# Two-layer hybrid trunk on one core: layers written out without barriers, opening transpositions one group late, output projection begun chunk by chunk

## The reference

```python
def _layer(x, mod, p, states):
    sh1, sc1, g1, sh2, sc2, g2, sh3, sc3, g3 = split(mod, 9)
    x = LN(ALPHA*x + 0.5*g1*swiglu(x*(1+sc1)+sh1, ffn_w_gu[0], ffn_w_down[0]))
    y, new_states = token_mixer(x*(1+sc2)+sh2, p, states)
    x = LN(ALPHA*x + g2*y)
    x = LN(ALPHA*x + 0.5*g3*swiglu(x*(1+sc3)+sh3, ffn_w_gu[1], ffn_w_down[1]))
    return x, new_states

# token_mixer: u = hin @ w_in feeds three branches (HGRN2, mLSTM, SSD); then
proj = einsum('blcr,crd->blcd', stack([y_hg, y_ml, y_mb]), w_branch)
y = einsum('blcd,de->ble', sigmoid(bg) * proj, w_out)

mod = silu(c) @ w_mod + b_mod     # 9 vectors of 1024 for each layer and token group
```

## Time and profile before

| | us |
|---|---|
| median of 3 runs | 2666.69 |
| the runs | 2666.21 to 2667.34 |
| the profiled execution | 2667.78 |
| span of that execution, first to last instruction | 2666.0 |

### The profile page before, as it was taken

The page is one execution under the profiler, slowest core; times in us unless marked ns, Lnnn a source line. Parts: engine busy times, 40 slices in busy tenths (PEclk is TensorE's granted clock), DMA queues, the critical chain, the costliest instruction groups (busy, mean ns, idle before and its releaser), DMA issues. The chain is left out here.

```text
span 2666.0 us, 36350 instructions
## 1 busy us (share of the span) xinstructions
PE 2397.3 (90%) x13210; PEld 2199.8 (83%) x13210; DVE 1201.2 (45%) x1684; ACT 1055.2 (40%) x1637; POOL 1472.8 (55%) x620
## 2 busy tenths in 40 slices
PE   4999989998889988999949999899988898889995
PEld 1999979787866787999949989788967678879995
DVE  3544137473643373542145431476637335554412
ACT  4443345333353625322244433642344445252222
POOL 3777645664364753655438775456634556445551
PEclk8999989999988998999979999899999899989998
DMA  6455333343243431443315543333323343323331
GB/s 228 145 172 173 124 97 135 111 135 119 77 134 122 157 95 64 146 127 115 130 47 182 166 153 124 109 119 127 119 97 109 135 134 127 103 89 127 125 118 55
DMA packets 96891, 331.26 MB, mean 124 GB/s; under 512 B 11248, under 2 KB 16624, under 8 KB 96368
## 3 DMA queue, kind: packets, MB, share of 16 engines
q1 hardware_dynamic: 89424, 320.41, 36.3%
q10 hardware_dynamic: 7328, 8.97, 1.0%
HBM read 325.14 MB, written 4.20 MB: 124 GB/s over the span
## 5 line engine op out<-in xcount | busy, mean ns | idle before, releaser
L540 POOL TENSOR_TENSOR wlo<-raw,whi 128x1024 fp32r<-128x1024 f32 (+2 forms) x616 | 1472.6, 2407 | 1144.9 <-ACT whi L1014 1112.0
L1014 ACT CAST whi<-raw 128x1024 fp32r<-128x1024 f32 (+1 forms) x616 | 632.3, 1038 | 838.5 <-DMA raw<-in_w_f 202.2
L573 PE MATMUL ps<-h_hi,whi 128*128 128x384 f32 x2176 | 748.8, 344 | 30.4 <-DVE xs L1620 13.3
L575 PE MATMUL ps<-h_hi,wlo 128*128 128x384 f32 x2176 | 737.3, 339 | 0.0
L574 PE MATMUL ps<-h_lo,whi 128*128 128x384 f32 x2176 | 736.6, 338 | 0.0
L573 PEld LDWEIGHTS ps<-h_hi,whi 128*128 128x128 f32 x2176 | 416.5, 191 | 49.2 <-issue 35.7
L574 PEld LDWEIGHTS ps<-h_lo,whi 128*128 128x128 f32 x2176 | 415.6, 191 | 6.3 <-issue 1.6
L575 PEld LDWEIGHTS ps<-h_hi,wlo 128*128 128x128 f32 x2176 | 415.1, 191 | 0.0
L573 PE MATMUL ps<-act_hi,whi 128*128 128x384 f32 x704 | 239.6, 340 | 11.8 <-DVEq L490 11.8
L575 PE MATMUL ps<-act_hi,wlo 128*128 128x384 f32 x704 | 239.3, 340 | 0.0
L574 PE MATMUL ps<-act_lo,whi 128*128 128x384 f32 x704 | 239.2, 340 | 0.0
(11 more groups left out here) (284 smaller groups left out, 3003.5 us busy)
## 6 DMA issues: line engine op xcount, KB each, us to landing
raw<-in_w_in SPq DMA_DIRECT2D x240, 512.0 KB, 3.5
raw<-in_w_f SPq DMA_DIRECT2D x136, 512.0 KB, 3.5
raw<-in_w_gu SPq DMA_DIRECT2D x88, 512.0 KB, 3.4
raw<-in_w_down SPq DMA_DIRECT2D x64, 512.0 KB, 3.4
raw<-in_w_down SPq DMA_DIRECT2D x32, 384.0 KB, 3.0
raw<-in_w_branch SPq DMA_DIRECT2D x24, 512.0 KB, 3.5
raw<-in_w_mod SPq DMA_DIRECT2D x16, 512.0 KB, 5.1
raw<-in_w_out SPq DMA_DIRECT2D x16, 512.0 KB, 3.4
```

Of the source, the lines that this page charges most:

```text
L540: nc.gpsimd.tensor_tensor(wlo[s][:, 0:w], raw[s][:, 0:w], whi[s][:, 0:w].bitcast(F32), ALU.subtract).then_inc(w_split, 1)
L573: mm(out, hi_, xh[:, xc, :], start=start and n == 0, stop=False)
L575: last = mm(out, lo_, xh[:, xc, :], start=False, stop=stop and n == len(chunks) - 1)
L1014: act.copy(whi[s][:, 0:w], raw[s][:, 0:w]).then_inc(w_hi, 1)
```

## The change

1. **Layers written out.** The loop over layers is a Python loop in each stream. The semaphores are not cleared; each wait adds what a layer has added before (`passed`). `layer_over` and the meeting ahead of it are gone. The third layer norm of layer 0 is followed at once by the modulated input of layer 1 with folded factors, as the other two are, and `ahead` runs across the border. The parameters of both layers are loaded at the start. y is stored chunk by chunk behind the affine step.
2. **Opening.** The rows of the four groups alternate between PSUM banks 0 and 1 and two row buffers. PE turns group g-1 behind the products of group g, ACT copies it after two more roundings. ACT also rounds the first four units of the layer in the opening, and a fifth after the second chunk's modulated input.
3. **Branches and output projection.** DVE makes `h_hi` straight from the sum, with the halving in it, for both chunks, then both `h_lo`. The factors (`adaln`) are made ahead of block 1, not of block 3. The first two units of the output projection go to banks 4 and 5, chunk by chunk, each chunk waiting only for its own `h_lo`.

```diff
-            with act.Fori(0, L) as l:
-                step.n = 0
-                act.dma_start(par[:, :], ins["par"][l]).then_inc(par_loaded, 16)
-                for k in range(AHEAD + 1):
-                    ahead(l, k - AHEAD)
-                act.wait_ge(md_go, 1)
-                for n in range(KC):
-                    modulated(0, n, mod[:, KC:2 * KC, :], mod[:, 0:KC, :])
+            for l in range(L):
+                now["l"] = l
+                if l == 0:
+                    act.wait_ge(md_go, 1)
+                    for n in range(KC):
+                        modulated(0, n, mod[:, KC:2 * KC, :], mod[:, 0:KC, :])
+                        if n == 1:
+                            ahead(l, 0)
                 ffn(l, 0, UF1)
...
                 layer_norm(l, 2)
-                meet(act, MEET["end", 0])
-                layer_over(act, l, "act")
...
@@ ACT, layer_norm
-                if j < 2:
-                    ahead(l, (UM, UF2)[j])
+                follows = j < 2 or l < L - 1
+                if follows:
+                    ahead(l, (UM, UF2, U_SPLIT)[j])
...
                 for n in range(KC):
                     act.wait_ge(ln_out, KC * j + n + 1 + passed(ln_out))
-                    if j < 2:
+                    if follows:
                         modulated(j + 1, n, gs, bs)
...
@@ PE, opening
-                mod_product(ps[0], m % NSET, m % 4).then_inc(w_used, 1)
-                if m % 4 == 3:
-                    pe.wait_ge(rows0_out, i(4) + (m // 4 + 1))
...
+            for m in range(U_MOD0):
+                pe.wait_ge(w_split, m + 1)
+                mod_product(ps[m // 4 % 2], m % NSET, m % 4).then_inc(w_used, 1)
+                if m % 4 == 3 and m > 3:
+                    first_turn(m // 4 - 1)
+            first_turn(U_MOD0 // 4 - 1)
...
@@ ACT, opening
+            for m in range(U_MOD0):
+                k = m + AHEAD
+                round_unit(k // NSET, k % NSET)
+                if m % 4 == 1 and m > 4:
+                    first_row(m // 4 - 1)
+            first_row(U_MOD0 // 4 - 1)
...
@@ PE, output projection
-                pe.wait_ge(br_hi, KC)
-                for k in range(U_OUT):
+                for c in range(KC):
+                    pe.wait_ge(br_hi, c + 1 + passed(br_hi))
+                    for m in range(2):
+                        if c == 0:
+                            unit_split(pe, l, u0 + m)
+                        last = block_product(ps[OUT_BANKS[m]][:, 0:T], u0 + m, h_hi, h_lo, [(c, c)], c == 0, c == KC - 1)
...
@@ DVE, branches
-                    if mblk == 3:
+                    if mblk == 1:
...
-                    ts(z[:, :, :], z[:, :, :], 0.5, None, ALU.mult).then_inc(br_z2, 1)
-                    dve.wait_ge(br_z2, mblk + 1)
-                    for j in range(2):
-                        k = 2 * mblk + j
-                        step(cp(h_hi[:, k, :], z[:, j, :]))
-                        step.done()
-                        tt(h_lo[:, k, :], z[:, j, :], h_hi[:, k, :].bitcast(F32),
-                           ALU.subtract).then_inc(br_hi, 1)
+                    ks = (2 * mblk, 2 * mblk + 1)
+                    for j, k in enumerate(ks):
+                        step(ts(h_hi[:, k, :], z[:, j, :], 0.5, None, ALU.mult))
+                    step.done()
+                    for j, k in enumerate(ks):
+                        stt(h_lo[:, k, :], z[:, j, :], 0.5, h_hi[:, k, :].bitcast(F32), ALU.mult,
+                            ALU.subtract).then_inc(br_hi, 1)
...
@@ SP, end
-            sp.wait_ge(layer_end, 9 * L)
-            sp.dma_start(outs["y"], x[:, :, :]).then_inc(stored, 16)
+            for n in range(KC):
+                sp.wait_ge(x_out, n + 1)
+                sp.dma_start(outs["y"][:, n, :], x[:, n, :]).then_inc(stored, 16)
```

473 lines of the change are left out of this document (239 added, 234 removed).

## The result

| | before | after |
|---|---|---|
| median, us | 2667.02 (4 runs, 2666.21 to 2670.44) | 2600.64 (4 runs, 2591.33 to 2605.78) |
| ratio to before | | 0.9745, 95% interval 0.9715 to 0.9775 |
| profiled execution, its span | 2667.78, 2666.0 | 2598.43, 2596.6 |
| mean granted clock | 0.943 | 0.955 |

What follows compares the result with a forecast made beforehand. PE, busy 90% of the span, was taken as the bound, so only its pauses and the slow clock behind them pay. Terms 25.1 + 14 + 24.6 + 5.5 = 69.2 us gave 2597.5, range 2589 to 2610.

Steps and rivals of the forecast that it cites:

- The border, 25.1: Between the layers: affine step, meeting, clearing, reload and five roundings leave the path, 25.1 us, bounds 22 and 27.
- The opening, 14: Start to first product: late turns and moved roundings let PE start at 52 to 53, not 66.45; 14 us, bounds 9, 18.
- 4.1 us more: Opening, behind the last row's copy: five roundings gone from there, 4.1 us on top of the 9 from an earlier copy.
- The rival of the weight ring: Opening: engines and DMA hang on each other through six buffers, gain 5 instead of 14, total 2606.5; chance 0.10.
- Branches and output projection, 24.6: Both layers: shorter waits and less lost clock around the branches, 12.3 us a layer, 24.6 in all, bounds 17 and 28.
- The output projection: Behind the branches: 36 matmuls with ready inputs cover PE's wait of 4.81, plus 1.7 of clock; gain 6.5 us a layer.
- Block 3: In the branches: without adaln PE's wait falls from 4.45 to 0.4, plus 1.8 of clock; gain 5.9 us a layer.
- Block 1: In the branches: adaln is new ahead of it; one blocked VectorE instruction as before, and 0.1 us more a layer.
- the first rival: VectorE late at block 1: blocked instructions and lost clock cost (2.1 + 1.8) x 2 = 8 us, total 2605; chance 0.10.
- The end, 5.5: Store of y: the last of eight small stores lands about 2.7 us after issue; 5.5 us gained, bounds 4 and 6.
- the prediction's own sign: Among PE's waits: a new entry over 3 us, above all for POOL's wlo in opening or border, would show it wrong.
- Straight code starves a sequencer: Rival on the written-out layers: late instruction fetch stops PE, 117 us over 87 packets, total 2715; chance 0.03.

Runs made afterwards that it cites:

- experiment 3: Two kernels, each the change with one edit: last row copied ahead of rounding unit 19 (2599.91 us), or VectorE's table work behind its last four units (2593.57 us).
- the change with 32 bytes: The change with everything from the feed-forward's buffers on moved up by 32 bytes in SBUF: 2597.97 us, ratio 0.9749 to before.
- experiments 1 and 2: The change with the opening's turns at once again (2612.49 us), and the change with the layer's five roundings behind the row copy again (first product at 54.23 us).
- with 672 bytes: The kernel before with the region from the feed-forward's buffers on moved up by 672 bytes per partition: 2670.33 us, 1.0014 times before.
- the kernel with four edits: The change with the last row copied before rounding unit 19, table work later, adaln inside block 0, arena moved 32 bytes: 2592.28 us, ratio 0.9726.
- experiment 7: The arena of activations moved by 32 bytes in the change (2597.97 us, ratio 0.9749), and by 672 in the kernel before (2670.33 us, 1.0014 times before).
- experiment 1: The change with the opening's turns put back, each right behind its own group of units, roundings still early: 2612.49 us.

## Why the prediction was right, step by step

**What bounds the kernel.** Right: PE executes the same matmuls, and the gain is PE's idle time and its clock. But 8.4 of the 14 us of clock came where no pause was removed (below).

**The border, 25.1.** Right to 0.1 us, since it was read off as the difference of two stretches of one trace. Of its parts one was not seen: the meeting itself costs ACT 0.10 us; the cost before lay in the affine step that all waited for and in clearing and jumping.

**The opening, 14.** Measured 10.67, inside the bounds of 9 to 18. The two parts add to 13; the 14 is from the start at 52 to 53, which came at 55.78. Products by 46 held (45.3). Two steps behind them did not: "that adds about one rounding, so the copy is near 47" (49.08: the load of unit 19 was late, and experiment 3 got 2.3 us back by going round it), and `mod` 2.7 behind the copy (4.2: an instruction blocked by POOL for 1.52). The first weighs more: in the change with 32 bytes that instruction took 0.17, and with the copy at 50.11 the start was still 55.97. More than a size was off in "4.1 us more": early rounding has no gain beside late turns, and costs 0.5 to 1.7. The sum added two parts that share ACT's stream and the ring; the square of experiments 1 and 2 shows that they do not add. The rival of the weight ring (5 us of gain) did not come, but it named the right resource.

**Branches and output projection, 24.6.** Measured 22.1 in two layers, inside 17 to 28. The output projection was sized too low: 8.3 a layer and not 6.5, the pause behind it costing more clock than the row of before had shown. Block 3 was sized too high and put down to the wrong cause: 5.9 predicted, while all that the new split and the moved `adaln` bring together is 3.7, and it comes from the shorter split. Block 1 was taken at no change; PE waits 1.63 and 1.80 there, where it waited 1.03. "I take one blocked instruction, as before" was right in the count, but `adaln`'s own five instructions, 1.1 us, were not covered. In layer 1 the wait also cost 1.5 us of clock. This is the first rival in small: it was priced at 2.1 + 1.8 a layer and came at 0.7, once with the clock.

**The end, 5.5.** Measured 6.88. The last store lands 2.26 us behind the last affine step, where 3 us had been forecast from a load of 256 KB (2.7), and 0.8 us came from ACT's affine steps starting sooner behind the layer norm's first matmul, most likely because those matmuls ran at the higher clock.

**What was not in the sum.** Three entries. The down projections' pace cost about 5.6 us, by a tile that moved the arena. The blocked `y_lo` ahead of the branches cost about 5.2. And the first layer norm and mixer, whose code is unchanged, took 7.3 us less, although 3.8 of `y_lo`'s price falls into this stage. In the kernels with the new border it took 545.4 to 551.0 us a layer, before 551.0, and with 672 bytes 552.2 and 552.6. The gain is the clock and nothing else: for 2758 matmuls PE was busy 499.86 and 500.01 us before, 493.73 and 497.79 in the change, and idle 1.0 us more in all. Why the clock was higher there stays open.

By the prediction's own sign, a new entry of over 3 us among PE's waits (3.21, twice), it missed a wait. It had named POOL's `wlo` as the likely one; it was a DVE instruction that POOL blocked. The four terms measured 64.8 and not 69.2, and the unforeseen entries made up for it. That the total is right to 3 us is therefore more than the terms deserve; their bounds, which all held but the end's (6 against 6.88), are what can be relied on.

**Straight code starves a sequencer.** It did not: 88 instruction packets in the whole run where there were 91 (44 and 43 of them in the two layers). The waits that the profile now puts down to "issue" are those of the layer norms, with their old length, and the one for `y_lo`. The Trainium skill, "Runtime: NRT & Kernel Launch", in its section on instruction fetch, has fetch run ahead sequentially; no run here speaks against it.

## What to carry to other kernels

Put a stretch that a change will copy beside the same stretch elsewhere in the same trace: the difference is the best estimate of all. When two edits move work on one engine's stream or through one ring, do not add their gains, since the work moved away from behind a point stands in front of it now. When a small VectorE instruction is on the path beside a GpSimd engine that works half the time, make GpSimd silent there or move the instruction to where VectorE waits anyway. And look for such instructions in code that the change does not touch, since it moves them against GpSimd's too.

## What the hardware showed beyond this

**The same pause, two clocks.** All layer norms have the same wait of 3.45 us ahead of their first matmul. Two of them in the change:

```profile
1010.00:1022.00 12.00, 3.01 (x9) 2.16 (x10) 9.51 (x16) 6.54 (x12) 2.34 (x1) 0.76 0.06 23
1307.00:1319.00 12.00, 3.55 (x6) 1.83 (x7) 8.18 (x13) 5.24 (x10) 2.34 (x1) 0.50 0.01 3
```

The first kept most of the full clock and its two matmuls took 0.91 us, the second was at 1.2 GHz and took 1.65. Before, all six took 1.65. It is no property of the change: with 672 bytes two layer norms of the kernel before kept part of the clock, and in the kernel with four edits none that a product follows did. Each that keeps the clock is 1.0 to 1.4 us shorter up to the next product. It may be one reason why the executions of the change scatter by 14 us and those of before by 4 to 9 within a session; only one execution of each kernel was traced, so that is not shown. In any case a single execution can't show an effect of 3 us by its time.

**An address changes matmul pace.** 0.1733 or 0.1760 us from matmul to matmul at full clock; moving the region that holds the moving operand switched it both ways, in all but one of the stages shifted in experiment 7.

**One instruction, two lengths.** The subtraction `y_lo` of 128x1536 took 1.74 us or 3.90, by what POOL was doing, and PE behind it ran 16, 20 or 29 matmuls in 5 us. The 29 are from experiment 1, layer 0: there `y_lo` took 1.75, PE waited 1.23, and branches and output projection took 90.0 us against 92.1 in its layer 1.
